# Column tiles of an expert block as blocks of ff columns, with VectorE turning the activations

## What is computed

```python
D_MODEL = 1024; SEQ = 256; D_FF = 2752; N_EXPERTS = 8; TOP_K = 2

def swiglu(x, w_gate, w_up, w_down):
    return (jax.nn.silu(x @ w_gate) * (x @ w_up)) @ w_down

def moe_ffn(x, w_router, w_gate, w_up, w_down):
    ...
    logits = (xt @ w_router).astype(F32)
    top_val, top_idx = lax.top_k(logits, TOP_K)
    top_w = jax.nn.softmax(top_val, axis=-1)
    ...
    yp = lax.map(run, (xp.reshape(n_blocks, MOE_BLOCK, D), block_e)).reshape(P, D)
    contrib = yp[dest] * w_s[:, None].astype(x.dtype)
    out = jnp.zeros((T, D), x.dtype).at[tok_s].add(contrib)
```

## Time and profile before

| | |
|---|---|
| median of 3 runs | 1300.02 us (1299.54 to 1300.07) |
| the profiled execution, its own time | 1300.21 us |
| its span | 1298.4 us |
| PE busy in the span | 97% |
| PEld, DVE, ACT, POOL | 66%, 46%, 32%, 3% |
| moved by DMA | 376.22 MB, 290 GB/s in the mean |
| clock of PE | full, but for 13.7 us ahead of block 0 and shorter stretches |

### The profile page before, as it was taken

How to read it: one execution, slowest core, us unless ns; L and a number is a source line. 1 busy time by engine, 2 the same in 40 slices (tenths; PEclk the granted TensorE clock), 3 DMA queues, 4 the chain that set the end, 5 groups by cost and what they waited for, 6 DMA issues and landing times.

```text
span 1298.4 us, 26040 instructions
## 1 busy us (share of the span) xinstructions
PE 1259.7 (97%) x11419; PEld 852.0 (66%) x11419; DVE 592.4 (46%) x1002; ACT 411.8 (32%) x735; POOL 43.8 (3%) x54
## 2 busy tenths in 40 slices
PE   6999999999999999999999999999999999999977
PEld 5787678888887887778855555555555555555533
DVE  6888987645544988987331212112122120211212
ACT  4444554643443444463311212111121111111100
POOL 0011010100000011010000000000000000000010
PEclk9999999999999999999799999999999999999999
DMA  9434433755543344446789999999999999999996
GB/s 344 158 135 158 162 125 138 273 180 189 185 146 130 138 155 162 163 185 254 315 306 395 419 386 367 413 418 419 418 418 420 394 366 423 417 420 416 420 419 243
DMA packets 58058, 376.22 MB, mean 290 GB/s; under 512 B 6322, under 2 KB 6914, under 8 KB 18004
## 3 DMA queue, kind: packets, MB, share of 16 engines
q1 hardware_dynamic: 56866, 370.17, 72.2%
q0 software_dynamic: 1072, 4.33, 1.0%
q10 hardware_dynamic: 2, 0.00, 0.0%
HBM read 371.07 MB, written 3.41 MB: 288 GB/s over the span
## 4 chain that ended last, share of the span: by engine, by line
PE 82%; DVE 4%; DMA 2%; ACT 1%; SPq 1%; issue 1%; POOL 0%; DVEq 0%; ACTq 0%
PE bank L2062 11%; PE bank L2081 11%; PE bank L1680 8%; PE bank L1681 8%; PE bank L2071 6%; PE bank L2120 5%; PE bank L1981 4%; PE bank L1730 4%; PE bank L2094 3%; PE bank L1958 3%; PE bank L2100 3%; PE bank L2111 3%; PE bank L2018 3%; PE bank L2145 2%; DMA ring<-in_moe 2%; DVE ys L1144 1%
## 5 line engine op out<-in xcount | busy, mean ns | idle before, releaser
L1155 DVE TENSOR_TENSOR w_lo<-raw,w_hi 128x2048 fp32r<-128x2048 f32 (+2 forms) x92 | 201.5, 2202 | 52.5 <-ACT w_hi L843 52.3
L1680 PE MATMUL bank<-w_hi,hT_hi 128*128 128x512 f32 (+1 forms) x528 | 209.3, 396 | 2.4 <-DVE hT_lo L1144 1.6
L1681 PE MATMUL bank<-w_hi,hT_lo 128*128 128x512 f32 (+1 forms) x528 | 205.1, 388 | 0.0
L843 ACT ACTIVATE w_hi<-raw 128x2048 fp32r<-128x2048 f32 (+2 forms) x92 | 169.1, 1847 | 88.5 <-PE bank L1730 42.7
L2062 PE MATMUL bank<-ring,hT_block 128*32 128x256 f32 (+1 forms) x2816 | 195.8, 374 | 0.0
L2081 PE MATMUL bank<-ring,hT_block 128*64 128x256 f32 (+1 forms) x1296 | 151.5, 377 | 5.2 <-DMA ring<-in_moe 5.1
L1561 DVE TENSOR_TENSOR both_k<-bank,odd_k 64x256 f32<-64x256 f32 (+1 forms) x44 | 18.1, 410 | 266.9 <-ACT odd_k L1077 266.9
L2062 PEld LDWEIGHTS bank<-ring,hT_block 128*32 128x32 f32 x2816 | 89.7, 110 | 68.6 <-issue 24.8
L1086 ACT ACTIVATE act_T<-bank 128x128 f32<-128x128 f32 (+1 forms) x88 | 26.8, 304 | 336.5 <-PE bank L2145 336.5
L2081 PEld LDWEIGHTS bank<-ring,hT_block 128*64 128x64 f32 x1296 | 89.1, 137 | 65.1 <-issue 19.1
L1565 DVE TENSOR_TENSOR act_moe<-silu_moe,bank 64x256 f32<-64x256 f32 (+1 forms) x88 | 36.7, 417 | 201.3 <-ACT silu_moe L1078 199.9
(11 more groups left out here) (286 smaller groups left out, 1507.8 us busy)
## 6 DMA issues: line engine op xcount, KB each, us to landing
ring<-in_moe SPq DMA_DIRECT2D x232, 1024.0 KB, 15.5
raw<-in_mix SPq DMA_DIRECT2D x56, 1024.0 KB, 4.8
raw<-in_dense SPq DMA_DIRECT2D x30, 1024.0 KB, 4.8
ring<-in_moe SPq DMA_DIRECT2D x16, 768.0 KB, 20.4
ring<-in_moe SPq DMA_DIRECT2D x8, 512.0 KB, 19.5
filters<-in_moe SPq DMA_DIRECT2D x2, 1024.0 KB, 9.9
gate_slots<-in_moe SPq DMA_DIRECT2D x2, 1024.0 KB, 11.1
ring<-in_moe SPq DMA_DIRECT2D x8, 256.0 KB, 17.2
```

What stands on the lines that cost most here:

```text
L843: nc.scalar.activation(HI[:, split_slot, 0:width], RAW[:, raw_slot, half:half + width], ACT.Copy)\
L1155: vec.tensor_tensor(LO[:, split_slot, 0:width], RAW[:, raw_slot, half:half + width], HI[:, split_slot, 0:width].bitcast(F32), ALU.subtract ...
L1680: mm(out_, left[0], right[0], start=start, stop=False)
L1681: mm(out_, left[1], right[1], start=False, stop=False)
```

## The change

Which weights are multiplied with which tokens stays the same; how the array is divided changes, for all blocks of layer 1.

- **Column tiles.** Each of four column tiles now holds the same 32 tokens and takes a quarter of the chunk's ff columns, gate beside up (64 and 64). Tokens go in groups of 32: two in a light block, three in a heavy one. The host lays the slabs out for it (`moe_slabs`). The down product has four tiles for four blocks of 256 output columns. Each matmul has 128 (gate and up) or 256 (down) moving columns, before 256 and 512.
- **Turning.** Tile q's partitions now hold 32 tokens by ff columns, so that 32x32 blocks turned in place are what the down product reads. DVE does it (`vec.transpose`), and PE's turning, ACT's copies and the sums of even and odd steps fall away.
- **PSUM.** A heavy block's gate and up take three banks for every chunk, and PE waits (`x_free`) until DVE has multiplied chunk c-1 before it begins chunk c. A light block alternates between two pairs.
- **Picks.** `pick_tokens` goes to chunk 6 (`PICK_AT`), in tiles of 32 or 64 columns; `hT_block` has two buffers, and ACT and DVE scale in chunk 6 too.
- **DMAs.** The last 64 rows of ff have a tile of their own (`last_rows`), with 16 rows on each quarter of the partitions, in four loads. The store of a block's output is four DMAs with pieces of 1 KB, before one with rows of 4 KB.
- **Start and end.** `hold_clock` is 3, 5 and 4, before 2, 4 and 2. The last spread works in four row tiles and DVE adds in eight pieces, before four.

```diff
+    tokens = region("tokens", KD * T, [[("hT_hi", [P, KD, T], F32R)], [("hT_block", [P, 2, KD, CAP], F32)]])
...
+    def picked_to(b, kd):
+
+        first = 6 if isinstance(b, int) and b and not is_heavy(b - 1) else 3
+        return PS[7 if kd // 4 else first][:, kd % 4 * CAP:(kd % 4 + 1) * CAP]
...
+    def groups(b):
+
+        return 3 if is_heavy(b) else 2
+
+    def tokens_of(b):
+
+        return HT[:, b % 2 if isinstance(b, int) else 0]
+
+    def x_banks(b, c):
+
+        return BANK[:, 0:3, :] if is_heavy(b) else BANK[:, c % 2 * 2:c % 2 * 2 + 2, :]
+
+    def gate_and_up(b, c):
+
+        width = (CHUNK if c < NCH else TAIL) // 4
+        return x_banks(b, c)[:, :, 0:width], x_banks(b, c)[:, :, width:2 * width]
+
+    def x_free(b, c):
+
+        behind = 1 if is_heavy(b) else 2
+        return (NCH + 1) * b + (Q_FIRST[1] + c + 1 - behind) if c >= behind else None
...
+                else:
+                    sp.wait_ge(slab_used, FFN_SLABS * b + first)
+                rows = (TAIL - P) // 4
+                for q in range(4):
+                    sp.dma_start(R["last_rows"][32 * q:32 * q + rows, :],
+                                 slabs["moe"][e, SLAB_AT[p] + q * rows * D:SLAB_AT[p] + (q + 1) * rows * D]
+                                 .rearrange("o (r n) -> (o r) n", n=D)).then_inc(last_rows_loaded, 16)
+                return
             to, width = weight(at, p), width_of(("ffn", 1), p)
             loaded = raw_loaded[slot_of(moe_place(at, p))]
...
-                    sp.dma_start(slot_y[START[b - 1]:START[b], :], Y[(b - 1) % 2][0:ROOM[b - 1], :]).then_inc(y_stored[(b - 1) % 2], 16)
+                    n = groups(b - 1)
+                    to = slot_y[START[b - 1]:START[b], :].rearrange("(t c) (q n) -> q c t n", t=n, q=4)
+                    for q in range(4):
+                        sp.dma_start(to[q], Y[(b - 1) % 2][32 * q:32 * q + 32, 0:n, :]).then_inc(y_stored[(b - 1) % 2], 16)
                 if at == 0 and p == 6:
                     slot = raw_slot(("mix", 1), MIX_SLABS - 1)
...
+            def activate(b, c, n):
+
                 act.wait_ge(slab_used, n + 1)
-                if heavy:
-                    nc.scalar.activation(R["odd_k"][0:64, 0:width], Y_BANKS[parity][64:128, 0:width], ACT.Copy).then_inc(odd_copied, 1)
-                nc.scalar.activation(R["silu_moe"][64:128, 0:width], X_BANKS[parity][0:64, 0:width], ACT.Silu).then_inc(silu_done, 1)
-                if heavy:
-                    act.wait_ge(both_summed, (NCH + 1) * heavy_number(b) + (c + 1))
-                    nc.scalar.activation(R["silu_moe"][32:64, 0:width], R["both_k"][0:32, 0:width], ACT.Silu).then_inc(last_silu_done, 1)
-
-            def copy_turned(b, c, rows):
-
-                act.wait_ge(turned, (NCH + 1) * b + (Q_FIRST[1] + c + 1))
-                nc.scalar.activation(R["act_T"][:, c % 2, :, 0:rows], PS[2][:, 0:2 * rows].rearrange("p (k t) -> p k t", k=2),
-                                     ACT.Copy).then_inc(act_copied, 1)
...
+            def gate_times_up(b, c):
+
+                n = groups(b)
+                done_by = (NCH + 1) * b + (Q_FIRST[1] + c + 1)
+                _, up = gate_and_up(b, c)
+                dve.wait_ge(silu_done, done_by)
                 if c == NCH:
-                    ins = vec.tensor_tensor(act[0:64, TAIL:CHUNK], silu[64:128, P:TAIL], up[:, P:TAIL], ALU.mult)
-                if heavy:
-                    dve.wait_ge(last_silu_done, done_by)
-                    ins = vec.tensor_tensor(act[64:96, 0:width], silu[32:64, 0:width], both[32:64, 0:width], ALU.mult)
-                    if c == NCH:
-                        ins = vec.tensor_tensor(act[64:96, TAIL:CHUNK], silu[32:64, P:TAIL], both[32:64, P:TAIL], ALU.mult)
-                ins.then_inc(act_done, 1)
...
             def moe_block(b, between):
 
-                heavy = is_heavy(b)
-                tokens_rear(b, CAP if heavy else LCAP)
                 if isinstance(b, int) and b:
-                    free = (y_stored[(b - 1) % 2], 16 * ((b - 1) // 2)) if b > 2 else None
-                    take_y(b - 1, Y[(b - 1) % 2], free, is_heavy(b - 1)).then_inc(y_taken, 1)
+                    free = (y_stored[(b - 1) % 2], 64 * ((b - 1) // 2)) if b > 2 else None
+                    take_y(b - 1, Y[(b - 1) % 2], free).then_inc(y_taken, 1)
                 for c in range(NCH + 1):
-                    gate_times_up(b, c, heavy)
+                    gate_times_up(b, c)
+                    if c == PICK_AT and isinstance(b, int) and b < NE - 1:
+                        tokens_rear(b + 1, ROOM[b + 1])
                     if c in between:
                         between[c]()
...
-                        hold_clock(2)
+                        hold_clock(3)
                     if kd % 2 == 0:
...
+                hold_clock(5)
                 pe.wait_ge(sem("router_parts"), 2)
                 pe.wait_ge(sem("sel_ready"), 1)
...
-                hold_clock(2)
+                hold_clock(4)
 
...
             def pick_tokens(b, room):
 
                 pe.wait_ge(psel_ready, b + 1)
+                cols = QUARTER if room == CAP else 2 * QUARTER
                 for kd in range(KD):
                     for tb in range(TB):
-                        ins = mm(picked_to(kd)[:, 0:room], X[:, tb, kd * P:(kd + 1) * P], R["psel"][:, tb, 0:room], start=tb == 0, stop=tb == TB - 1)
+                        for q in range(0, P, cols):
+                            ins = mm(picked_to(b, kd)[q:q + cols, 0:room], X[:, tb, kd * P + q:kd * P + q + cols], R["psel"][:, tb, 0:room],
+                                     start=tb == 0, stop=tb == TB - 1)
                     if kd % 4 == 3:
...
+            def gate_up_moe(b, at, k0, nk, c):
+
+                width, tokens = (CHUNK if c < NCH else TAIL) // 2, tokens_of(b)
                 for k in range(nk):
                     kd = k0 + k
-                    for u in range(2):
-                        col = (2 * k + u) * width
-                        ins = mm(X_BANKS[parity][64 * u:64 * u + 64, 0:width], HT[:, kd, 0:LCAP], at[:, col:col + width],
-                                 start=kd == 0, stop=kd == KD - 1)
+                    for t in range(groups(b)):
...
+            def down_moe(b, at, c, tiles, start=False, stop=False):
+
+                for i, j in enumerate(tiles):
+                    for t in range(groups(b)):
+                        for q in range(4):
+                            ins = mm(Y_BANKS[t][32 * q:32 * q + 32, 0:CHUNK],
+                                     R["act_T"][:, c % 2, 64 * t + 32 * j:64 * t + 32 * j + 32],
+                                     at[:, i * D + q * CHUNK:i * D + (q + 1) * CHUNK], start=start and j == 0, stop=stop)
                 ins.then_inc(slab_used, 1)
...
-            def turn_moe(b, c, rows):
-
-                pe.wait_ge(act_done, (NCH + 1) * b + (Q_FIRST[1] + c + 1))
-                cols = 32 if rows == CAP else LCAP
-                for k in range(2):
-                    for q in range(0, P, cols):
-                        ins = mm(PS[2][q:q + cols, k * rows:(k + 1) * rows], R["act_moe"][0:rows, k * P + q:k * P + q + cols],
-                                 IDENT[0:rows, 0:rows], start=True, stop=True)
-                ins.then_inc(turned, 1)
...
+                    gate_up_moe(b, loaded(b, part, turns), 2 * part, 2, 0)
                 for c in range(1, NCH + 1):
-                    p, parity, width = 3 * c + 1, c % 2, CHUNK if c < NCH else TAIL
-                    gate_up(loaded(b, p, turns), 0, 4, parity, width)
-                    turn_moe(b, c - 1, rows)
-                    gate_up(loaded(b, p + 1, turns), 4, 4, parity, width)
+                    p = 3 * c + 1
                     if c == 1 and isinstance(b, int) and b:
                         pe.wait_ge(y_taken, 2 * b)
-                    if c == NCH and isinstance(b, int) and b < NE - 1:
+                    if x_free(b, c) is not None:
+                        pe.wait_ge(act_done, x_free(b, c))
+                    gate_up_moe(b, loaded(b, p, turns), 0, 4, c)
+                    gate_up_moe(b, loaded(b, p + 1, turns), 4, 4, c)
+                    if c == PICK_AT and isinstance(b, int) and b < NE - 1:
                         pick_tokens(b + 1, ROOM[b + 1])
-                    pe.wait_ge(act_copied, (NCH + 1) * b + c)
-                    down(loaded(b, p + 2, turns), 1 - parity, c == 1, c == NCH)
-                turn_moe(b, NCH, rows)
+                    pe.wait_ge(act_turned, (NCH + 1) * b + c)
+                    down_moe(b, loaded(b, p + 2, turns), c - 1, (0, 1), start=c == 1)
                 if amid:
                     amid()
-                pe.wait_ge(act_copied, (NCH + 1) * b + (NCH + 1))
-                last_at = loaded(b, 35, turns)
-                down(loaded(b, 34, turns), 0, False, True, False)
-                (heavy_down_last if heavy else light_down_last)(last_at)
```

(21 more changed lines are left out.)

252 lines of the change are left out of this document (99 added, 153 removed).

## The result

The changed kernel takes 1422.93 us in the median of four runs (1418.12 to 1431.54), the kernel before 1299.97 in the same comparison: a ratio of 1.0954, with a 95% interval of 1.0898 to 1.1010. The forecast was 1290.5, the range 1282 to 1303. The loss is 123 us where a gain of 10 was expected.

The account below looks back on a forecast made before the run. The prediction took weight loads, plus time without free slots, as the bound. From 1300.2 us it summed -12.8 (heavy blocks), -3.0 (behind block 0's start), -4.2 (start), +8.0 (fetches), +1.0 and +0.3 to 1289.5, rounded to 1290.5; range 1282 to 1303.

Parts of the forecast that it names:

- What bounds the kernel before: Expert blocks from 643 us on: loads set the end, all bytes at full rate plus 30.4 us lost without free slots.
- PE's share: PE's own time in expert blocks: heavy chunk 7.74 us for 8.09, heavy block 87.3, light one 58.6.
- VectorE's turning: Turning on DVE in each chunk: taken at 0.35 us, hidden behind a light block's down product, so nothing added.
- The new wait for the banks: Heavy blocks: chunk 1 waits until ACT and DVE are through with chunk 0, 1.1 us a block.
- The fetches: More matmuls need 80 more instruction fetches on the full DMA engines, 0.11 us each: +8.0 us, between +5 and +9.
- Rival (a): Expert blocks: PE can't be fed instructions fast enough; 1345 us at 17 ns each, 1439 at 20.3; 12%.
- the prediction's estimate from the 20 cycles: Issue floor of an instruction on PE, by the skill's 20 cycles at 1.2 GHz: 16.7 ns.
- The start: Ahead of block 0: longer held matmuls and faster picks, perhaps at full clock, let it begin earlier: -4.2 us.
- The stores of 1 KB pieces and the single loads: Output stores in 1 KB pieces and the loads of `last_rows`: +1 us, from 0 to +3.
- the sum: Whole kernel: the terms add up to -10.7 us against 1300.2, giving 1289.5, rounded to 1290.5 us.

Follow-up runs that it names:

- the fastest kernel: whole_rows with the picks of heavy blocks in tiles of 64 columns, as in light ones: 1292.46 us, 0.9965 of the kernel before.
- the paired kernel: pairs_all with a quarter of the bytes in the slab loads of blocks 1 to 7: 1243.47 us.
- small_loads: The changed kernel, but from block 1 on slab loads, except those of the first four slabs, bring only a quarter of their columns: 1283.61 us.
- pairs_all: The changed kernel with chunks 0 to 9 in pairs, so gate and up matmuls have 256 moving columns: 1303.06 us, 1.0040 of the kernel before.
- whole_rows: pairs_all with the last 64 rows of ff as one load of 128 rows, half zeros, not four of 16: 1294.62 us, 0.9984 of the kernel before.

## Why the prediction was wrong, step by step

- **What bounds the kernel before: right.** The loads do. The profile of the fastest kernel shows it from the other side: with PE's own heavy block at 88 us the stretch from 760 to 820 us moves 413 GB/s, where it was 369.
- **PE's share: right.** Heavy chunk 7.83 us for 7.74, blocks of 88 and 60 us for 87.3 and 58.6 (the blocks in the paired kernel, the only one whose PE was left nearly free). VectorE's turning took 0.345 us in the mean for the 0.35 taken. The new wait for the banks took 0.85 to 0.89 us a heavy block for the 1.1 taken.
- **The fetches: the step that failed.** "So 80 fetches more. They use the same full DMA engines": they were counted (79 came) and priced as traffic, at 0.11 us each, +8.0. Nowhere was it asked how soon one of them arrives. 480 instructions in 7.74 us ask for 256 every 4.1 us, and in the trace of before the closest two such packets in a full stretch of the expert blocks lay 6.4 us apart (6.43 at 417 GB/s; 5.43 once at 393). That number was there to be read; it is the nearest row to a demand of 4.1. It sets no limit, since PE never stood there, but taken as one it would have given heavy blocks of 5,536 / 256 x 6.4 = 138 us beside full engines, as a bound for the slower side. The changed kernel shows the limit: 6.1 us beside full engines, and blocks of 106 to 114 us, since the engines didn't stay full.
- **Rival (a): the right outcome on the wrong grounds.** "PE can't be fed" had 12%, priced by nanoseconds an instruction, and was held small because a burst of 32 instructions went at 10.6 ns. That burst was evidence on the pace of issue, which was never the limit (13.6 ns over 384 instructions, in small_loads). The limit is supply, by blocks of 256. The measured heavy block comes to 20.3 ns an instruction (112.58 us / 5,536), which is by accident the upper price of the rival, 1439 us.
- **The Trainium skill** ("Runtime: NRT & Kernel Launch", Instruction fetch mechanics) says that the sequencer fetches the next 16 KiB block of 256 instructions while it executes the current one. The traces agree with that rule (94 of 98 pauses at one place of a block of 256). It also says that the cost is mostly hidden, because issue, at some 20 cycles each, is slower than the refill. Here both parts fail: 139.1 us of pauses at fetches, and 13.6 ns an instruction, where the prediction's estimate from the 20 cycles is 16.7.
- **The start: right in size, wrong in kind.** Block 0 began at 637.47 us, 5.5 earlier than in the profiled execution of before, where -4.2 was taken. But 4.5 of it the kernel before reaches by itself in most executions on the other chips (11 of 17 on one). A gain over one execution that had bad luck isn't a gain over the kernel.
- **"The stores of 1 KB pieces and the single loads": mis-sized.** +1 us was taken, 0 to +3. The stores cost nothing that shows. The loads of 16 rows cost 7 to 8 us (pairs_all against whole_rows), after the bytes that whole rows add are paid for. What they cost in the changed kernel no run shows; slow 4 KB packets are in its trace too (a tenth take 241 ns or more).
- **What the sum leaves.** From 1290.5 to 1422.9 are 132 us, and the pauses are 142.7. Part of these falls into time that was waited for weights anyway, and the clock, at 0.50 for 37.5 us, takes up to 19; the runs don't split these further.
